# A 544-column pitch for the split activations, on a boundary of 256 bytes, in a hybrid decoder trunk

## The chip, the cores and the metric

The kernel runs on one core of one Trainium2 chip. The metric is the time of one execution on the device in microseconds. Of three runs of the kernel before, the median is 2366.6 us (2359.94, 2366.6 and 2373.5). No other core works beside it.

## The reference

A causal decoder trunk of two layers over 512 tokens with 16 learned tokens in front (528 positions, model width 1024, float32). Each layer is a SwiGLU feed-forward block, a token mixer, and a second SwiGLU block, each between two RMS norms:

```
h = concatenate([meta, x])
for layer in range(2):
    f = swiglu(rms_norm(h, nw[0]), w_gate, w_up, w_down)      # 1024 -> 2816 -> 1024
    h = h + 0.5 * rms_norm(f, nw[1])
    hn = rms_norm(h, nw[2])
    mix = even_mixer(hn) if layer == 0 else odd_mixer(hn)
    h = h + rms_norm(mix, nw[3])
    f = swiglu(rms_norm(h, nw[4]), w_gate, w_up, w_down)
    h = h + 0.5 * rms_norm(f, nw[5])
return h[:, 16:]
```

The even mixer is sliding-window attention beside a gated DeltaNet, with one input projection (1024 to 2824) and one output projection (1024 to 1024). The odd mixer is a gated linear attention in chunks (input 1024 to 3088, output 1024 to 1024). The four feed-forward blocks and the four projections hold most of the arithmetic.

## The kernel before, in words

**Layout.** The residual `h` lies transposed: 128 model columns on the partitions, eight such tiles (`DT` = 8), and the 528 tokens (`TOK`) along the row. All dense products are out = W^T h: a 128x128 block of weights is loaded into TensorE, and the tokens are streamed past it.

**Split operands.** TensorE reads both operands in the format fp32r. For precision each operand is kept as a high and a low part. The activations lie in `x_hl` (2 parts x 8 tiles x 528 columns), the hidden activations of a feed-forward block in `acts` (2 parts x 22 tiles x 528 columns), the weights in `w_hl` (a ring of four slots, 2 parts each). For each tile `kt` of the contraction `products` (L521) makes three products: high weights with high activations, high with low, low with high. Each is made once for every half of the tokens: columns 0 to 263 and 264 to 527. So one `kt` is six matmuls of 264 columns:

```
for part, moved in ((0, 0), (0, 1), (1, 0)):
    lhs = core.w_hl[:, slot.ring, part, w_tile * P:(w_tile + 1) * P]
    for b, (t0, n) in enumerate(halves(phase.cols)):
        op = pe.matmul(out, lhs, moving[:, moved, kt, t0:t0 + n], ...)
```

Where the first 16 tokens are no longer needed (layer 1 from the output projection on), a `kt` is three matmuls of 512 columns, from column 16 on.

**Slots.** A slot is one tile of 128 output columns (half of one in the down projection): 8 `kt` of `x_hl` in the gate, up, input and output projections, 11 `kt` of `acts` in each half of the down projection. SyncE loads its weights into `stage` (L510), ScalarE writes the high part (L446), VectorE the low part (L453), three slots ahead of TensorE. Semaphores count slots; each engine walks the same list of phases. ScalarE and VectorE also take each result out of PSUM: L970 to L989 and L793, L797 for the gate and up projection, which leave `acts`; L826, L829 for the down projection, which leave `f_down`; L968 for the input projections.

**Norms.** Between the phases `scalar_norm` and `vector_norm` work tile by tile: the scaled result of the phase before (`f_down` or `f_mix`) is added to `h` (L926), ScalarE writes the high part of `h` times the norm's weights into `x_hl` (L762), VectorE the low part (L917), and GpSimd adds squares (L1041).

**Places in SBUF.** The tiles are allocated one behind the other. `x_hl` starts at byte 100,000 of each partition (`x_at`), which is 160 beyond a multiple of 256, and its rows lie 528 x 4 = 2112 bytes apart, which is 64 beyond a multiple of 256. The low part starts 8 x 2112 = 16,896 bytes behind the high part, a multiple of 256. `f_down` lies over the high part of `x_hl` with the same pitch. The arena starts at byte 133,792, again 160 beyond a multiple of 256. It holds `acts`, and in other stages `f_mix`, the mixers' tiles, the constants' rows and `rows_x` and `rows_out`, the input and the output as they are in memory. The low part of `acts` starts 22 x 2112 bytes behind the high part, 128 beyond a multiple of 256. The weights in `w_hl` start at byte 33,408 and their blocks lie 512 bytes apart, so every block starts 128 beyond a multiple of 256.

Of the kernel before, what the change touches and what calls it, by code (L numbers as in the profile page):

```python
# [29 lines left out]
F32R = mybir.dt.float32r  # L30

P = 128
META = 16
SEQ = 512
TOK = META + SEQ
# [6 lines left out]
DT = D // P  # L42
# [23 lines left out]
SCALAR_LOADS = 6  # L66
VEC_ROWS = CONV * 3 * DH + 4 + 2 + 1
HALF = TOK // 2
FULL = "full"
TAIL = "tail"  # L70

# [57 lines left out]
class Phase:  # L129


    def __init__(self, kind, layer, slots, cols, before, ffn=None):
        self.kind, self.layer, self.slots, self.cols, self.ffn = kind, layer, slots, cols, ffn
        self.slot0 = before["slots"]

        self.partial = 0 if layer else slots - 1
        self.lead = 1 if kind == "in" and layer else 0
        self.evac0 = before["evac"]
        self.f0 = before["f"]
        self.x0 = before["x"]  # L140
        self.a0 = before["a"]
        before["slots"] += slots
        if kind in ("gu", "in"):
            before["evac"] += slots
        if kind == "gu":
            before["a"] += slots // 2
        if kind in ("down", "out"):
            before["f"] += DT
# [32 lines left out]
def plan(stop=None):  # L181
# [6 lines left out]
    def norm(layer, post, pre, half, cols, last=False):  # L188
        nonlocal norms, sums
        steps.append(("norm", Norm(layer, post, pre, half, cols, h0=norms * DT, x0=n["x"], sum0=sums,  # L190
                                   pair=(n["slots"] + RING - 1) % RING, last=last,
                                   sum_pair=(n["slots"] + (RING - 1 if half else RING - 2)) % RING)))
        norms += 1
        sums += (post is not None) + (pre is not None)
        if pre is not None:
            n["x"] += DT

    norm(0, None, 0, False, FULL)
    for layer in range(2):
        cols = FULL  # L200
        for ffn in range(2):
            if ffn:
                cols = TAIL if layer else FULL
            steps.append(("dense", Phase("gu", layer, 2 * FT, cols, n, ffn=ffn)))
# [7 lines left out]
            norm(layer, 1, 2, True, cols)  # L212
            steps.append(("dense", Phase("in", layer, (ODD_TILES if layer else EVEN_TILES) + 1, FULL, n)))
            steps.append(("mix", Mix(layer, n["x"], n["evac"], n["slots"])))
            n["x"] += DT
            steps.append(("dense", Phase("out", layer, DT, TAIL if layer else FULL, n)))
            if stop == (layer, "mix"):
                norm(layer, 3, None, False, TAIL if layer else FULL, last=True)
                return steps
# [4 lines left out]
def halves(cols):  # L224

    if cols == TAIL:
        return [(META, SEQ)]
    return [(0, HALF), (HALF, HALF)]


def token_cols(tile, cols):

    if cols == TAIL:
        return tile[:, META:TOK]
    return tile.rearrange("p (a b) -> p a b", a=2)
# [22 lines left out]
class Core:  # L258


    def __init__(self, nc, ctx, steps):
        self.nc, self.steps = nc, steps
        self.phases = [s for kind, s in steps if kind == "dense"]
        last = [s for kind, s in steps if kind == "norm"][-1]
        self.h_total = last.h0 + DT

        def sb(name, shape, dt=F32):
            return ctx.enter_context(nc.sbuf_tensor(name, shape, dt))

        def sem(name):  # L270
            return ctx.enter_context(nc.semaphore(name))

        self.h = sb("h", [P, DT, TOK])
        self.w_hl = sb("w_hl", [P, RING, 2, FH * P], F32R)
        self.stage = sb("stage", [P, 2, FH * P])
        self.rinv = sb("rinv", [P, TOK])
        self.sq_sum = sb("sq_sum", [P, TOK])
        self.t_gate = sb("t_gate", [P, TOK])
        self.t_up = sb("t_up", [P, TOK])
        self.ident = sb("ident", [P, P])  # L280
        self.ones = sb("ones", [P, P])
        self.norm_cols = sb("norm_cols", [P, 12 * DT])
        self.vec_cols = sb("vec_cols", [P, 64])
        self.heads = sb("heads", [P, QH + 2 * DH])
        self.eps = sb("eps", [P, 4])
        self.by_token = sb("by_token", [P, 2, 6])
        self.x_at = (nc.sbuf_base + 31) // 32 * 32
        self.x_hl = sb("x_hl", [P, 2, DT, TOK], F32R)
        self.arena = (nc.sbuf_base + 31) // 32 * 32
        self.acts = sb("acts", [P, 2, FT, TOK], F32R)  # L290
        self.psum = ctx.enter_context(nc.psum_tensor("psum", [P, 8, 512], F32))


        self.f_down = self.at("f_down", [P, DT, TOK], self.x_at)
        self.f_mix = self.at("f_mix", [P, DT, TOK], self.arena)

        at = self.arena
        def rows_at(name, rows, width):
            nonlocal at
            buf = self.at(name, [rows, width], at)  # L300
            at += (4 * width + 31) // 32 * 32
            return buf

        self.rows_x = rows_at("rows_x", P, NBLK * D)
        self.rows_meta = rows_at("rows_meta", META, D)
        self.rows_norm = rows_at("rows_norm", 12 * DT, P)
        self.rows_vec = rows_at("rows_vec", VEC_ROWS, P)
        self.table = rows_at("table", BUCKETS + 1, QH)
        self.bucket_hot = rows_at("bucket_hot", BUCKETS + 1, V_ALL)
        self.bias_row = rows_at("bias_row", QH, V_ALL)  # L310
        self.rows_x = self.rows_x[:].rearrange("p (b d) -> p b d", b=NBLK)
        self.rows_out = self.at("rows_out", [P, NBLK, D], self.arena)

        self.w_hi = sem("w_hi")
        self.w_lo = sem("w_lo")
        self.slot_used = sem("slot_used")
        self.scaled = sem("scaled")
        self.gate_silu = sem("gate_silu")
        self.act_full = sem("act_full")
        self.act_hi = sem("act_hi")  # L320
        self.act_lo = sem("act_lo")
        self.f_out = sem("f_out")
        self.sq_made = sem("sq_made")
        self.sq_added = sem("sq_added")
        self.sum_ready = sem("sum_ready")
        self.root_ready = sem("root_ready")
        self.rinv_ready = sem("rinv_ready")
        self.f_scaled = sem("f_scaled")
        self.f_scaled_pool = sem("f_scaled_pool")
        self.inverse_ready = sem("inverse_ready")  # L330
        self.spread_set = sem("spread_set")
        self.spread_ready = sem("spread_ready")
        self.spread_copied = sem("spread_copied")
        self.table_set = sem("table_set")
        self.h_new = sem("h_new")
        self.x_hi = sem("x_hi")
        self.x_lo = sem("x_lo")
        self.consts_in = sem("consts_in")
        self.vectors_in = sem("vectors_in")
        self.consts_set = sem("consts_set")  # L340
        self.cols_ready = sem("cols_ready")
        self.cols_flip = sem("cols_flip")
        self.tok_in = sem("tok_in")
        self.tok_flip = sem("tok_flip")
        self.bias_stored = sem("bias_stored")
        self.out_flip = sem("out_flip")
        self.out_left = sem("out_left")
        self.out_right = sem("out_right")
        self.out_stored = sem("out_stored")
        self.w_landed = [sem("w_landed_0"), sem("w_landed_1")]  # L350
        self.sem = sem
        self.tables = 0
        self.even = Even(self)
        self.odd = Odd(self)
        self.proj = [self.even.proj, self.odd.proj]
# [366 lines left out]
def bank_cols(core, pair, cols):  # L722
    if cols == TAIL:
        return core.psum[:, 2 * pair, 0:SEQ]
    return core.psum[:, 2 * pair:2 * pair + 2, 0:HALF]

# [218 lines left out]
def vector_dense(core, dve, phase):  # L945
    k = core

    def step(i, u):
# [9 lines left out]
        if phase.kind == "in":  # L958
# [5 lines left out]
            if slot.peeled:  # L964
                tile = k.proj[phase.layer][0:rows, at, :]
                src = k.psum[0:rows, 2 * slot.pair:2 * slot.pair + 2, 0:HALF]
                rinv = token_cols(k.rinv[0:rows, :], phase.cols)
# [1504 lines left out]
```

## Time and profile before

| | |
|---|---|
| median of three runs | 2366.6 us |
| profiled execution, its own time | 2361.65 us |
| its span, first to last instruction | 2359.9 us |
| TensorE busy with matmuls | 2250.8 us, 95% |
| VectorE, ScalarE, GpSimd busy | 1037.5, 749.6, 213.7 us |
| read from HBM | 175.64 MB, 75 GB/s |
| mean granted clock of TensorE | 0.976 of full |

Matmuls overlap in the records: one of 264 columns lasts some 284 ns from its start to its end, but the next one starts some 120 ns after it. So the rate is read from starts and counts, and not from the mean duration. A start is given to 0.01 us. A window on the time axis shows each instruction that is under way in it, with its true start.

### The profile page before, as it was taken

The page shows a single profiled execution, that of the slowest core. Times are in us where ns is not written, and L with a number is a line of the kernel's source. Part 1 is how long each engine was busy: PE and PEld are TensorE (multiplying, and loading weights), DVE is VectorE, ACT ScalarE, POOL GpSimd, SP SyncE. Part 2 cuts the span into 40 slices and gives each one's busy share as a digit, 9 for nine tenths or more (in the row PEclk, how much of TensorE's full clock was granted, in tenths as well). Part 3 has the DMA queues.
Part 4 walks back from the last instruction along what each step waited for, and adds up shares of the span by engine and source line. Part 5 has one row for each costly group of instructions (what it writes and reads, how often), then busy time and mean ns, then how long its engine had stood idle before and what let it go on. Part 6 is the DMA issues. An engine that isn't in the chain of part 4 may idle for free.

```text
span 2359.9 us, 38299 instructions
## 1 busy us (share of the span) xinstructions
PE 2250.8 (95%) x16046; PEld 2080.9 (88%) x16046; DVE 1037.5 (44%) x1298; ACT 749.6 (32%) x1103; POOL 213.7 (9%) x185
## 2 busy tenths in 40 slices
PE   7999999899969999999998999999899998999997
PEld 6999999788839889999998999999899776888885
DVE  5444422665454546444314544431564337444322
ACT  3322322344422433222222322222352454222321
POOL 2000000300044030000002000000200012000001
PEclk9999999998989999999999999999999999999998
DMA  3333332321100022333431333332132122333420
GB/s 104 98 89 90 104 108 72 74 66 46 46 9 2 1 72 81 89 89 89 117 88 36 95 92 89 96 111 72 40 92 72 45 75 60 98 89 98 119 86 36
DMA packets 347333, 179.02 MB, mean 76 GB/s; under 512 B 15657, under 2 KB 345680, under 8 KB 347246
## 3 DMA queue, kind: packets, MB, share of 16 engines
q1 hardware_dynamic: 346032, 175.30, 25.8%
q0 software_dynamic: 880, 2.34, 0.5%
q8 instruction: 65, 1.06, 0.2%
q14 instruction: 22, 0.18, 0.0%
q10 hardware_dynamic: 334, 0.14, 0.0%
HBM read 175.64 MB, written 2.12 MB: 75 GB/s over the span
## 4 chain that ended last, share of the span: by engine, by line
PE 89%; DVE 7%; ACT 2%; DMA 1%; issue 1%; POOL 0%; DVEq 0%; SPq 0%; ACTq 0%; POOLq 0%
PE psum L521 77%; DVE h L926 3%; DVE x_hl L917 1%; PE psum L1318 1%; ACT x_hl L762 1%; PE psum L1665 1%; PE psum L1681 1%; PE psum L1679 1%; PE psum L1337 1%; PE psum L646 1%; DMA stage<-even_w_in 0%; PE psum L2192 0%; PE psum L637 0%; PE psum L1351 0%; PE psum L1303 0%
## 5 line engine op out<-in xcount | busy, mean ns | idle before, releaser
L521 PE MATMUL psum<-x_hl,w_hl 128*128 128x264 f32 (+1 forms) x10272 | 1428.8, 301 | 42.7 <-DVE x_hl L917 39.4
L521 PEld LDWEIGHTS psum<-x_hl,w_hl 128*128 128x128 f32 x10272 | 1354.6, 191 | 118.4 <-issue 31.7
L453 DVE TENSOR_TENSOR w_hl<-stage,w_hl 128x1024 fp32r<-128x1024 f32 (+1 forms) x304 | 400.3, 1317 | 440.7 <-ACT w_hl L446 440.4
L521 PE MATMUL psum<-acts,w_hl 128*128 128x264 f32 (+1 forms) x3696 | 508.7, 300 | 0.0
L521 PEld LDWEIGHTS psum<-acts,w_hl 128*128 128x128 f32 x3696 | 484.6, 188 | 23.7
L446 ACT ACTIVATE w_hl<-stage 128x1024 fp32r<-128x1024 f32 (+1 forms) x304 | 338.5, 1114 | 226.1 <-PE psum L521 158.5
L976 DVE TENSOR_TENSOR t_up<-psum,rinv 128x528 f32<-128x528 f32 (+1 forms) x88 | 61.9, 703 | 306.6 <-PE psum L521 306.5
L797 ACT ACTIVATE acts<-t_up 128x528 f32 (+3 forms) x88 | 56.7, 644 | 401.1 <-DVE t_up L979 401.1
L970 DVE TENSOR_TENSOR t_gate<-psum,rinv 128x528 f32<-128x528 f32 (+1 forms) x88 | 61.8, 703 | 184.5 <-PE psum L521 184.4
L793 ACT ACTIVATE t_gate<-t_gate 128x528 f32<-128x528 f32 (+1 forms) x88 | 56.6, 643 | 249.5 <-DVE t_gate L970 249.5
L1037 POOL COPY sq_sum<-t_gate 128x528 f32<-128x528 f32 (+1 forms) x12 | 9.8, 818 | 1268.9 <-ACT t_gate L826 1262.3
L1041 POOL TENSOR_TENSOR sq_sum<-sq_sum,t_up 128x528 f32<-128x528 f32 (+1 forms) x42 | 59.3, 1411 | 226.8 <-ACT t_up L826 192.2
L1041 POOL TENSOR_TENSOR sq_sum<-sq_sum,t_gate 128x528 f32<-128x528 f32 (+1 forms) x36 | 51.4, 1428 | 219.4 <-ACT t_gate L826 189.9
L979 DVE TENSOR_TENSOR t_up<-t_up,t_gate 128x528 f32<-128x528 f32 (+1 forms) x88 | 62.0, 704 | 9.5
L989 DVE TENSOR_TENSOR acts<-t_up,acts 128x528 f32 (+3 forms) x88 | 61.4, 698 | 2.8 <-ACT acts L797 2.8
L826 ACT ACTIVATE t_gate<-psum 128x528 f32<-128x528 f32 (+1 forms) x24 | 14.6, 609 | 140.0 <-PE psum L521 140.0
L762 ACT ACTIVATE x_hl<-h,norm_cols 128x528 fp32r<-128x528 f32 (+1 forms) x48 | 35.2, 732 | 69.2 <-DVE h L926 69.2
L826 ACT ACTIVATE t_up<-psum 128x528 f32<-128x528 f32 (+1 forms) x24 | 14.5, 606 | 128.1 <-PE psum L521 128.1
L917 DVE SCALAR_TENSOR_TENSOR x_hl<-h,norm_cols,x_hl 128x528 fp32r<-128x528 f32 (+1 forms) x48 | 45.0, 949 | 19.1 <-ACT x_hl L762 19.1
L968 DVE TENSOR_TENSOR odd_proj<-psum,rinv 128x528 f32<-128x528 f32 (+1 forms) x25 | 17.5, 704 | 72.7 <-PE psum L521 72.7
L968 DVE TENSOR_TENSOR even_proj<-psum,rinv 128x528 f32<-128x528 f32 (+1 forms) x23 | 16.1, 705 | 64.6 <-PE psum L521 64.5
L926 DVE TENSOR_TENSOR h<-h,f_down 128x528 f32<-128x528 f32 x24 | 40.5, 1689 | 0.1
(311 smaller groups left out, 1342.1 us busy)
## 6 DMA issues: line engine op xcount, KB each, us to landing
stage<-ffn_w_gate SPq DMA_DIRECT2D x88, 512.0 KB, 3.8
stage<-ffn_w_up SPq DMA_DIRECT2D x88, 512.0 KB, 3.8
stage<-ffn_w_down SPq DMA_DIRECT2D x64, 704.0 KB, 4.6
stage<-odd_w_in SPq DMA_DIRECT2D x24, 512.0 KB, 3.8
stage<-even_w_in SPq DMA_DIRECT2D x18, 512.0 KB, 3.8
stage<-even_w_out SPq DMA_DIRECT2D x8, 512.0 KB, 3.6
stage<-odd_w_out SPq DMA_DIRECT2D x8, 512.0 KB, 3.8
rows_x<-x SPq DMA_DIRECT2D x1, 2048.0 KB, 10.4
```

The costliest lines, as they stand in the source:

```text
L446: act.activation(weights(core.w_hl[:, slot.ring, 0, :], *kind), weights(core.stage[:, slot.stage, :], *kind), ACT.Copy).then_inc(core.w_hi, 1)
L453: dve.tensor_tensor(weights(core.w_hl[:, slot.ring, 1, :], *kind), weights(core.stage[:, slot.stage, :], *kind), weights(core.w_hl[:, slot ...
L521: op = pe.matmul(out, lhs, moving[:, moved, kt, t0:t0 + n], start=first and part + moved == 0, stop=last and part == 1)
L762: act.activation(k.x_hl[:, 0, kt, norm.t0:TOK], tile, ACT.Copy, scale=k.norm_cols[:, col:col + 1]).then_inc(k.x_hi, 1)
L797: act.activation(token_cols(tile_at(k.acts[:, 0], t), phase.cols), token_cols(k.t_up[:, :], phase.cols), ACT.Copy).then_inc(k.act_hi, 1)
L917: dve.scalar_tensor_tensor(k.x_hl[:, 1, kt, t0:TOK], k.h[:, kt, t0:TOK], k.norm_cols[:, col:col + 1], k.x_hl[:, 0, kt, t0:TOK].bitcast(F32 ...
L926: dve.tensor_tensor(k.h[:, kt, t0:TOK], k.h[:, kt, t0:TOK], f[:, kt, t0:TOK], ALU.add).then_inc(k.h_new, 1)
L970: dve.tensor_tensor(token_cols(k.t_gate[:, :], phase.cols), src, rinv, ALU.mult).then_inc(k.scaled, 1)
L976: dve.tensor_tensor(up, src, rinv, ALU.mult).then_inc(k.scaled, 1)
L979: dve.tensor_tensor(up, up, gate, ALU.mult).then_inc(k.act_full, 1)
L989: dve.tensor_tensor(token_cols(tile_at(k.acts[:, 1], t), phase.cols), up, hi, ALU.subtract)\
L1041: pool.tensor_tensor(k.sq_sum[:, t0:TOK], k.sq_sum[:, t0:TOK], buf, ALU.add).then_inc(k.sq_added, 1)
```

## The change

The rows of `x_hl` are allocated 544 columns long (`PITCH`), of which the first 528 are used. 544 x 4 = 2176 bytes is 128 beyond a multiple of 256. A tile `x_gap`, which nothing reads or writes, fills the partition up to the next multiple of 256 bytes (`LINE`), so `x_hl` starts at byte 100,096. It takes 2 x 8 x 2176 = 34,816 bytes, a multiple of 256, so the arena starts on one too, at byte 134,912. `f_down` gets the pitch of `x_hl`, over which it lies. `acts` keeps its pitch of 528 columns. The weights stay where they are.

```
+PITCH = 544
+LINE = 256
...
+        self.x_gap = sb("x_gap", [P, (-nc.sbuf_base) % LINE // 32 * 8])
         self.x_at = (nc.sbuf_base + 31) // 32 * 32
-        self.x_hl = sb("x_hl", [P, 2, DT, TOK], F32R)
+        self.x_hl = sb("x_hl", [P, 2, DT, PITCH], F32R)[:, :, :, 0:TOK]
         self.arena = (nc.sbuf_base + 31) // 32 * 32
         self.acts = sb("acts", [P, 2, FT, TOK], F32R)
         self.psum = ctx.enter_context(nc.psum_tensor("psum", [P, 8, 512], F32))
 
 
-        self.f_down = self.at("f_down", [P, DT, TOK], self.x_at)
+        self.f_down = self.at("f_down", [P, DT, PITCH], self.x_at)[:, :, 0:TOK]
         self.f_mix = self.at("f_mix", [P, DT, TOK], self.arena)
```

Where the operands of the dense matmuls start, in bytes beyond a multiple of 256 (`kt` counted from the first row):

| | before | after |
|---|---|---|
| `x_hl`, first half, kt = 0, 1, 2, 3 | 160, 224, 32, 96 | 0, 128, 0, 128 |
| `x_hl`, second half | 192, 0, 64, 128 | 32, 160, 32, 160 |
| `x_hl`, 512 columns from column 16 | 224, 32, 96, 160 | 64, 192, 64, 192 |
| `acts` high, first half, kt = 0, 1, 2, 3 | 160, 224, 32, 96 | 0, 64, 128, 192 |
| `acts` high, second half | 192, 0, 64, 128 | 32, 96, 160, 224 |
| `acts` high, 512 columns from column 16 | 224, 32, 96, 160 | 64, 128, 192, 0 |

The low part of `x_hl` starts at the same places as the high part, the low part of `acts` 128 bytes further.

## Rows read from the trace of the kernel before

**Rows 1.** The page: TensorE's line, then the chain that ended last, by engine and line

```profile
PE 2250.8 (95%) x16046; PEld 2080.9 (88%) x16046; DVE 1037.5 (44%) x1298; ACT 749.6 (32%) x1103; POOL 213.7 (9%) x185
PE 89%; DVE 7%; ACT 2%; DMA 1%; issue 1%; POOL 0%; DVEq 0%; SPq 0%; ACTq 0%; POOLq 0%
```

**Rows 2.** That chain in order of time, merged: start us, us, what, xcount

```profile
50.01 368.10 PE psum L521 x3024
...
1305.64 368.11 PE psum L521 x3024
...
1980.67 351.58 PE psum L521 x1512
```

**Rows 3.** Stretches: length, busy us of engines (count), granted clock, DMA share, GB/s

```profile
901.00:1269.10 368.10, 368.10 (x3027) 368.10 (x3028) 138.22 (x148) 102.20 (x121) 8.63 (x7) 1.00 0.32 94
1269.10:1305.64 36.54, 27.56 (x181) 24.57 (x179) 26.81 (x27) 13.94 (x23) 13.70 (x10) 0.86 0.00 1
```

**Rows 4.** Groups of instructions, shapes apart: L521, count, busy us, mean ns, idle before

```profile
L521 PE MATMUL psum<-x_hl,w_hl 128*128 128x264 f32 x9024 | 1134.1, 288 | 35.0 <-DVE x_hl L917 31.9 <-DVE w_hl L453 1.0 <-DVE odd_proj L968 0.9
L521 PE MATMUL psum<-acts,w_hl 128*128 128x264 f32 x3168 | 385.8, 284 | 0.0
L521 PE MATMUL psum<-x_hl,w_hl 128*128 128x512 f32 x1248 | 294.7, 397 | 7.6 <-DVE x_hl L917 7.5 <-ACT rinv L732 0.2
L521 PE MATMUL psum<-acts,w_hl 128*128 128x512 f32 x528 | 123.0, 394 | 0.0
```

**Rows 5.** Instructions by time, TensorE: first matmuls of kt 0 to 4, one slot of `x_hl`

```profile
1405.00 0.40 PE L521 MATMUL psum<-x_hl,w_hl 128*128 128x264 f32 x2
1405.72 0.40 PE L521 MATMUL psum<-x_hl,w_hl 128*128 128x264 f32 x2
1406.45 0.42 PE L521 MATMUL psum<-x_hl,w_hl 128*128 128x264 f32 x2
1407.19 0.41 PE L521 MATMUL psum<-x_hl,w_hl 128*128 128x264 f32 x2
1407.92 0.40 PE L521 MATMUL psum<-x_hl,w_hl 128*128 128x264 f32 x2
```

**Rows 6.** The same for `acts`: first matmuls of kt 4, 6 and 8

```profile
1175.53 0.41 PE L521 MATMUL psum<-acts,w_hl 128*128 128x264 f32 x2
...
1176.99 0.41 PE L521 MATMUL psum<-acts,w_hl 128*128 128x264 f32 x2
...
1178.45 0.41 PE L521 MATMUL psum<-acts,w_hl 128*128 128x264 f32 x2
```

**Rows 7.** The same, `x_hl` with 512 columns: kt 0, 4, 6, 7, 8

```profile
2075.51 0.63 PE L521 MATMUL psum<-x_hl,w_hl 128*128 128x512 f32 x2
...
2078.30 0.62 PE L521 MATMUL psum<-x_hl,w_hl 128*128 128x512 f32 x2
...
2079.68 0.64 PE L521 MATMUL psum<-x_hl,w_hl 128*128 128x512 f32 x2
2080.39 0.62 PE L521 MATMUL psum<-x_hl,w_hl 128*128 128x512 f32 x2
2081.08 0.63 PE L521 MATMUL psum<-x_hl,w_hl 128*128 128x512 f32 x2
```

**Rows 8.** One line of ScalarE: duration ns min/median/max, first and last start

```profile
L762 ACT ACTIVATE x_hl<-h,norm_cols x48: 719/737/742, 22.6 to 1975.7; 128x528 fp32r<-128x528 f32 x40, 128x512 fp32r<-128x512 f32 x8
```

**Rows 9.** By time, one tile of a norm: VectorE's writes and GpSimd's add

```profile
1281.37 0.77 DVE L917 SCALAR_TENSOR_TENSOR x_hl<-h,norm_cols,x_hl 128x528 fp32r<-128x528 f32 x1 [0.19 <-ACT x_hl L762]
...
1281.95 1.36 POOL L1041 TENSOR_TENSOR sq_sum<-sq_sum,t_up 128x528 f32<-128x528 f32 x1 [0.91 <-ACT t_up L767]
...
1282.05 1.82 DVE L926 TENSOR_TENSOR h<-h,f_down 128x528 f32<-128x528 f32 x1
```

**Rows 10.** The start: landing of `x` (issued at 0.75 us), TensorE's first instruction

```profile
rows_x<-x SPq DMA_DIRECT2D x1, 2048.0 KB, 10.4
12.35 0.40 PE L658 MATMUL psum<-ident,rows_norm 96*128 96x96 f32 x1 [12.35 <-DMA heads<-dn_dt_bias]
```

## The prediction

> **What bounds the kernel now.** I read the page first. TensorE is busy 95% of the span, VectorE 44% and ScalarE 32%, and 89% of the chain that ended last runs over TensorE [rows 1]. The chain in order of time shows where: in four stretches it does not leave the dense matmuls of L521 at all. Three of these stretches hold 3024 matmuls of 264 columns each in 368.1 us (the first and the last of the three are in [rows 2]). The fourth holds 1512 matmuls of 512 columns in 351.58 us. That is 3 x 368.1 + 351.6 = 1455.9 us, 62% of the span. In such a stretch the granted clock is 1.00, the higher of the two levels (2.4 GHz), TensorE is busy all the time, and DMA works a third of it [rows 3]. So nothing there is waited for: the time is the number of matmuls times the distance from one to the next. Any change in that distance passes straight into the span. Between the stretches VectorE sets the time (26.81 of 36.54 us in the norm of [rows 3], with TensorE waiting for its tiles).
>
> The shapes kept apart give the counts [rows 4]: from `x_hl` 9024 matmuls of 264 columns and 1248 of 512, from `acts` 3168 and 528. The mean durations there overlap and are no distance. The distances come from starts. One slot of `x_hl` starts its `kt` at 1405.00, 1405.72, 1406.45, 1407.19 and 1407.92 [rows 5]: 0.72, 0.73, 0.74 and 0.73 us for six matmuls each, 2.92 us for four `kt`, 121.7 ns for a matmul. Four `kt` of `acts` also take 2.92 us (1175.53 to 1178.45), 1.46 for each two [rows 6]. With 512 columns four `kt` take 2.79 us (2075.51 to 2078.30), 232.5 ns for a matmul; of the next four, two take 1.38 together, then one 0.71 and one 0.69 [rows 7]. So the `kt` are not equal, though the instructions of each have the same shapes. What differs from one `kt` to the next is where the rows start, and that repeats after four of them. The trace thus has a hint that the start of a row plays a part, of 0.02 us in 0.73.
>
> **The change, part by part.** No instruction is added or taken away, and no wait, semaphore or transfer changes. What changes is the addresses of `x_hl`, `f_down` and all of the arena. So the sum has one kind of term: the number of instructions with a moved operand, times what the move is worth.
>
> *`x_hl`, 264 columns.* 9024 matmuls are 9024 / 6 = 1504 `kt`. Before, a quarter of them start at each of (160, 192), (224, 0), (32, 64) and (96, 128), first and second half, and take 0.72, 0.73, 0.74 and 0.73 us, as `kt` 0 to 3 of [rows 5]. After, half start at (0, 32) and half at (128, 160). The trace has neither pair. It has the four single places, though: the pair (0, 32) lies between (224, 0) and (32, 64), so I give it (0.73 + 0.74) / 2 = 0.735. The pair (128, 160) lies between (96, 128) and (160, 192), so it gets (0.73 + 0.72) / 2 = 0.725. Their mean is 0.730, that of before, and the term is 0. The bounds, by the nearest rows: all at the cheapest, 1504 x (0.72 - 0.73) = -15 us; all at the dearest, 1504 x (0.74 - 0.73) = +15 us. I take 0, since one new pair stands beside the dearest place and the other beside the cheapest.
>
> *`x_hl`, 512 columns.* 1248 / 3 = 416 `kt`, mean 0.697, dearest 0.71 and cheapest 0.69 [rows 7]. All starts of before are 32 beyond a multiple of 64, all starts of after (64, 192) are multiples of 64. With no row at such a start I take 0, with bounds from -3 to +5 us.
>
> *`acts`.* The pitch stays, and after as before each of four starts serves a quarter of the `kt`; the places only move by 96 bytes. Here the pairing of high and low part differs from that in `x_hl` (the low part starts 128 further on), and still four `kt` cost the same 2.92 us [rows 5, 6]. The mean over a full round of starts thus looks indifferent to how they follow each other. I take 0. The bounds, with half a hundredth of a microsecond of reading error on 3168 / 6 + 528 / 3 = 704 `kt`: -3.5 to +3.5 us.
>
> *The writers of `x_hl` and `f_down`.* ScalarE's L762 writes rows at all four starts, and its 48 durations lie within 719 to 742 ns, with both shapes in them [rows 8]. A shift of 12 ns in all 48 would be 0.6 us. VectorE's writes have a larger spread, but its cause stands beside them: the addition L926 takes 1.82 us where GpSimd's L1041 has begun 0.10 us before it and lasts 1.36, while the write of `x_hl` (L917), which meets no such neighbour, takes 0.77 [rows 9]. Addresses have no part in that. I take 0, from -1 to +1.
>
> *DMA.* `rows_x` lies in the arena. Its transfer is issued at 0.75 us and lands 10.4 us later, at 11.2, while TensorE's first instruction waits for a constant until 12.35 [rows 10]. A faster landing is hidden. A slower one is hidden up to 1.2 us, and costs its excess beyond that. The weights' loads go to `stage`, which is not moved, and TensorE waits for none of them in the long stretches. Term 0.
>
> *The mixers' tiles* move by 96 bytes with the arena and keep their shapes and pitches. All matmuls outside L521 are 16046 - 13968 = 2078, with other shapes; 1 ns on each is 2 us. Term 0, from -2 to +2.
>
> **The sum.** 0 + 0 + 0 + 0 + 0 + 0. The profiled execution took 2361.65 us for its span of 2359.9, which is 4.95 us under the median of the runs, 2366.6. I forecast that median again, to the full microsecond: 2366 us. The bounds added up are -25 and +27 us.
>
> **The rivals.**
>
> *Blocks (faster).* A read could cost by the aligned blocks of 64 bytes that it touches. 264 columns (1056 bytes) touch 17 at any multiple of 32, before and after. 512 columns (2048 bytes) touch 33 from a start that is 32 beyond a multiple of 64, and 32 from a multiple of 64. The two distances would then give (232.5 - 121.7) / 16 = 6.9 ns for a block, and the change saves one on each of 1248 + 528 = 1776 matmuls: -12.3 us, 2354 us. For it: the distances fit such a law, and all 512-column matmuls get an aligned start. Against it: they fit a price by column as well, since there are only two widths. The SBUF page of the Trainium skill ("SBUF — State Buffer", "Specifications (TRN2)") gives lines of 16 bytes. By that rule 512 columns touch as many lines before as after, and nothing is gained. No row here shows a line's size.
>
> *Kind places (faster).* The pairs (0, 32) and (128, 160) could both cost as the cheapest `kt`, 0.72: -15 us, 2351 us. For it: the pair that is that cheap now, (160, 192), contains one of the new places. Against it: the places 32 and 64 make the dearest pair, and 32 now serves a quarter of all reads instead of an eighth.
>
> *All of it alignment (much faster).* At 2.4 GHz 264 columns are 110.0 ns and 512 are 213.3, and the rows show 121.7 and 232.5. Were the surplus due to starts off a multiple of 256 and gone after: 12192 x 11.7 + 1776 x 19.2 = 177 us less, 2190 us. Against it: the `kt` of `x_hl` whose second half starts exactly at 0 takes 0.73, as much as one with starts at 96 and 128 and more than the one at (160, 192). On its own the page of the Trainium skill "TensorE: Matmul & The Clock Gate" ("Back-to-back issue gap") gives N/2.4 + 2.5 ns for the distance of warm matmuls, 112.5 and 215.8 ns here. The rows are 9.2 and 16.7 ns above it. By that rule the most that aligned starts could bring is 12192 x 9.2 + 1776 x 16.7 = 142 us, an estimate.
>
> *A clash that stays (slower).* A read of the tokens runs while the next block of weights is read, and all weights start at 128. A pair of starts could stand badly to that, as (32, 64) does, the dearest of [rows 5]. Of the new starts, 32 is in every second `kt`, and 128, on which the weights start too, leads the others. If both new pairs are dear for such a reason, all `kt` of 264 columns take 0.74: +15 us. The same on 512 columns, all at the dearest 0.71: 416 x 0.013 = +5 us. Together +20 us, 2386 us. For it: a pitch of 128 beyond 256 uses two places where 64 used four, so a bad one is no longer averaged out. Against it: 64 may be the bad one in its pair, and it is used no more in the halves; and 128 in second place costs 0.73, no more than the mean. It passes the line of 0.5% when the mean `kt` of 264 columns goes beyond 0.738 us.
>
> **How the numbers follow.** Of a change in this kernel 0.5%, some 12 us, can be told from none. No change has 0.61. Blocks has 0.09, kind places 0.09, all alignment 0.02; together 0.20 for faster. The clash that stays has 0.19. The range from 2348 to 2384 holds the forecast, the runs' own spread of 7 us to each side, blocks, kind places, and of the clash what makes one of the two new pairs dear, and most of what makes both. It leaves out the much faster case and the full clash with the 512 columns in it. The bounds of the unknown costs reach further, but only if every row falls on the same side.
>
> **What the profile after would show.** Right: the three stretches of 3024 matmuls at 368 us and the one of 1512 at 352, each within 1.5 us, and four `kt` of `x_hl` at 2.92 us, now with a pattern that repeats after two. Norm stretches stay at 36.5 us. Blocks: `kt` of 512 columns at 0.677 us and unchanged ones of 264. Kind places: 2.88 us for four `kt` of `x_hl`, and 2.92 for `acts`. Clash: 2.95 us or more for four `kt` of `x_hl`. I am wrong if the distance in `x_hl` leaves 121 to 122.5 ns, or if that of `acts` moves although each of its starts still serves a quarter.

## The result and the profile after

The changed kernel is slower by 0.39%: 2373.27 us median against 2364.14 before, eleven runs each, ratio 1.0039 with a 95% interval from 1.0023 to 1.0054. I had forecast 2366 us and no change. The time lies in the stated range, but the change is clear of the noise and is none that I called likeliest.

The page of the kernel after, TensorE's line and the chain by engine, as [rows 1] of before:

```profile
PE 2258.9 (96%) x16046; PEld 2091.0 (88%) x16046; DVE 1037.9 (44%) x1298; ACT 749.3 (32%) x1103; POOL 214.0 (9%) x185
PE 89%; DVE 7%; ACT 2%; DMA 1%; issue 0%; POOL 0%; ACTq 0%; DVEq 0%; SPq 0%; POOLq 0%
```

The counts are the same and only TensorE is busy longer, by 8.1 us. The chain in order of time (start us, us, what), as [rows 2], says where:

```profile
49.51 371.07 PE psum L524 x3024
...
904.75 371.07 PE psum L524 x3024
1312.44 371.04 PE psum L524 x3024
...
1989.90 348.56 PE psum L524 x1512
```

The same 3024 matmuls take 371.07 us instead of 368.10, three times, while the 1512 of 512 columns take 348.56 instead of 351.58. In sum +5.9 us in the long stretches. The stretch between the first two and the norm behind the second, by length, busy time of the engines, granted clock, DMA share and GB/s, as [rows 3]:

```profile
904.75:1275.82 371.07, 371.07 (x3027) 371.07 (x3028) 138.36 (x148) 102.00 (x121) 8.65 (x7) 1.00 0.32 93
1275.82:1312.44 36.62, 28.41 (x180) 25.61 (x179) 26.80 (x27) 13.94 (x23) 13.69 (x10) 0.81 0.01 1
```

The granted clock is 1.00 in both kernels and the other engines do what they did, so no wait and no lower clock lengthens the stretch. The norm is as long as before (36.62 and 36.54 us). What has changed is the distance from one matmul to the next. Here are the first matmuls of `kt` 0 to 4 of a slot of `x_hl`, as [rows 5]:

```profile
1413.11 0.41 PE L524 MATMUL psum<-x_hl,w_hl 128*128 128x264 f32 x2
1413.85 0.40 PE L524 MATMUL psum<-x_hl,w_hl 128*128 128x264 f32 x2
1414.59 0.41 PE L524 MATMUL psum<-x_hl,w_hl 128*128 128x264 f32 x2
1415.33 0.40 PE L524 MATMUL psum<-x_hl,w_hl 128*128 128x264 f32 x2
1416.07 0.41 PE L524 MATMUL psum<-x_hl,w_hl 128*128 128x264 f32 x2
```

Four `kt` take 2.96 us, each 0.74; before they took 2.92 (0.72, 0.73, 0.74, 0.73). With 512 columns, as [rows 7] but `kt` 0 to 4:

```profile
2083.82 0.62 PE L524 MATMUL psum<-x_hl,w_hl 128*128 128x512 f32 x2
2084.51 0.62 PE L524 MATMUL psum<-x_hl,w_hl 128*128 128x512 f32 x2
2085.20 0.62 PE L524 MATMUL psum<-x_hl,w_hl 128*128 128x512 f32 x2
2085.89 0.62 PE L524 MATMUL psum<-x_hl,w_hl 128*128 128x512 f32 x2
2086.58 0.62 PE L524 MATMUL psum<-x_hl,w_hl 128*128 128x512 f32 x2
```

Four take 2.76 us, before 2.79. The starts repeat so exactly that a slot is known to some nanoseconds. This is what a slot takes where TensorE waits for nothing (133 slots of `x_hl` with 264 columns and 45 with 512 in each trace), from its start to that of the next; `count` is the number of all such slots in the kernel:

```
slot                                before      after     count   difference
x_hl, 264 columns (48 matmuls)     5.840 us   5.920 us     188     +15.0 us
x_hl, 512 columns (24)             5.573      5.520         52      -2.8
acts, 264, halves of a tile (66)   8.026, 8.028   8.029, 7.991   24 each   -0.8
acts, 512, halves of a tile (33)   7.675, 7.678   7.626, 7.624    8 each   -0.8
sum                                                                  +10.6
```

Not every slot is the common one: in the kernel after 124 of the 133 take 5.920 us, and five in a row, in the input projection of layer 1, take 5.867. With the mean of the 133 the first term is +14.5 us. The medians of the two kernels differ by 9.1 us. The two profiled executions differ by only 4.7 us in their spans: 188 counts also the slots of the input projections, where TensorE waits for others in between and part of a longer slot is hidden, and the stretches with waits vary by a few microseconds from run to run.

### The profile page after: what moved, and what is told of

Its sections match the earlier page's. It is cut to its first block, busy times and chain, and to the rows that moved or that the text cites. A ratio compares the mean times of both kernels' runs of the same rounds, so it can differ in the third digit from the quotient of the medians.

```text
span 2364.6 us, 38299 instructions
## 1 busy us (share of the span) xinstructions
PE 2258.9 (96%) x16046; PEld 2091.0 (88%) x16046; DVE 1037.9 (44%) x1298; ACT 749.3 (32%) x1103; POOL 214.0 (9%) x185
## 4 chain that ended last, share of the span: by engine, by line
PE 89%; DVE 7%; ACT 2%; DMA 1%; issue 0%; POOL 0%; ACTq 0%; DVEq 0%; SPq 0%; POOLq 0%
PE psum L524 77%; DVE h L929 3%; DVE x_hl L920 1%; PE psum L1321 1%; ACT x_hl L765 1%; PE psum L1668 1%; PE psum L1684 1%; PE psum L649 1%; PE psum L1682 1%; PE psum L1340 1%; DMA stage<-even_w_in 1%; PE psum L1306 0%; PE psum L2195 0%; PE psum L640 0%; PE psum L1354 0%
## 5 line engine op out<-in xcount | busy, mean ns | idle before, releaser
L829 ACT ACTIVATE t_up<-psum 128x528 f32<-128x528 f32 (+1 forms) x24 | 14.5, 605 | 127.4 <-PE psum L524 127.4
## 6 DMA issues: line engine op xcount, KB each, us to landing
rows_x<-x SPq DMA_DIRECT2D x1, 2048.0 KB, 10.6
```

## The experiments

My theory after this result, "places": the distance between two matmuls depends on where in 256 bytes the reads of the tokens start. Two rivals: the neighbours at work in SBUF stretch it, or it is the pitch as such, two places in place of four.

**The matmuls by themselves.** A kernel that only streams matmuls, in the order of `products`, from tiles at chosen bytes (`s` is the start of the first read beyond a multiple of 256, the second read follows 1056 bytes on):

```
+for part, moved in ((0, 0), (0, 1), (1, 0)):
+    for b, (s, n) in enumerate(kt):
+        pe.matmul(psum[:, b, 0:n], wt[w][:, part, (i % 8) * P:(i % 8 + 1) * P], tile[:, at:at + n], ...)
```

> Leaves the whole trunk out: it only streams matmuls of the changed kernel's kind (three products for each of 8 kt, two halves of 264 columns, every weight block 128 bytes beyond a multiple of 256) from tiles that start at chosen bytes. Its output is not the trunk's. Theory 'places': the distance between matmuls is a function of where the reads of the tokens start, modulo 256 bytes, and of nothing else in the kernel. Then the case with the starts of the kernel before takes 5.84 us for 48 matmuls and the case with those of the kernel after 5.92, as in the two traces, with no other engine at work. Rival 'neighbours': the distance is stretched by what VectorE, ScalarE and DMA do in SBUF at the same time; then both cases come out alike here, and under 5.84. Of the cases with one pair of starts throughout I expect by 'places' (0, 32) and (128, 160) at 5.90 to 5.95 and some pair at or below 5.80. The cases with the weights at 0 instead of 128 tell whether the place counts by itself or against the weights' place: if against it, the row of eight pairs is the same but turned by 128 bytes (0 and 128 change places); if by itself, it is the same row unturned. 256 and 272 columns in place of 264 and 264: by 'places' the second read then starts where the first does, modulo 256.

The trace of that kernel by time: start, us, and what TensorE does. `before_x` and `after_x` have the starts of the two kernels, with the weights at 128:

```profile
50.17 6.00 PE L100 MATMUL psum<-before_x,w_mid 128*128 128x264 f32 x48
56.01 6.04 PE L100 MATMUL psum<-after_x,w_mid 128*128 128x264 f32 x48
61.89 46.68 PE L100 MATMUL psum<-pair_x,w_mid 128*128 128x264 f32 x384
```

From start to start 5.84 us for the layout of before, exactly as in the kernel, and 5.88 for that of after: in its second half the `kt` take 0.74 us each as in the kernel, in the first half they are still finding that pace. VectorE and GpSimd do nothing here, and ScalarE next to nothing, so the neighbours are out. Then eight starts, each for 48 matmuls, first with the weights at 128 (`w_mid`) and then at 0 (`w_zero`); each row is the first of a start:

```profile
61.89 0.41 PE L100 MATMUL psum<-pair_x,w_mid 128*128 128x264 f32 x2
67.81 0.40 PE L100 MATMUL psum<-pair_x,w_mid 128*128 128x264 f32 x2
...
79.35 0.40 PE L100 MATMUL psum<-pair_x,w_mid 128*128 128x264 f32 x2
85.12 0.40 PE L100 MATMUL psum<-pair_x,w_mid 128*128 128x264 f32 x2
90.88 0.40 PE L100 MATMUL psum<-pair_x,w_mid 128*128 128x264 f32 x2
...
102.53 0.41 PE L100 MATMUL psum<-pair_x,w_mid 128*128 128x264 f32 x2
108.41 0.41 PE L100 MATMUL psum<-pair_x,w_zero 128*128 128x264 f32 x2
114.17 0.40 PE L100 MATMUL psum<-pair_x,w_zero 128*128 128x264 f32 x2
...
125.83 0.41 PE L100 MATMUL psum<-pair_x,w_zero 128*128 128x264 f32 x2
131.71 0.41 PE L100 MATMUL psum<-pair_x,w_zero 128*128 128x264 f32 x2
137.63 0.41 PE L100 MATMUL psum<-pair_x,w_zero 128*128 128x264 f32 x2
...
149.18 0.40 PE L100 MATMUL psum<-pair_x,w_zero 128*128 128x264 f32 x2
154.95 0.41 PE L100 MATMUL psum<-same_x,w_mid 128*128 128x264 f32 x2
```

The differences of the starts, the rows left out included, in microseconds for 48 matmuls:

```
start of the first read      0     32    64    96    128   160   192   224
weights at 128             5.92  5.76  5.77  5.77  5.76  5.80  5.86  5.88
weights at 0               5.76  5.80  5.86  5.88  5.92  5.78  5.77  5.77
```

The second line is the first turned by 128, to 0.02 us. So a start is neither good nor bad by itself: what counts is how far beyond the weights' start it lies, modulo 256. Best are the same place and the 96 bytes below it: the starts 32, 64, 96 and 128 all settle at 120 ns for a matmul, which is 288 cycles at 2.4 GHz. On the weights' place itself every single matmul of the settled half follows after 120 ns. Worst is 128 beyond (5.92 us). The changed kernel has every second `kt` of `x_hl` exactly there, its first reads at 0 against weights at 128. One half of my expectation failed: I had (128, 160) at 5.90 or more, and by itself it is among the best, 0.720 us for a `kt`. In the changed kernel, between two `kt` at (0, 32), it takes 0.738. So a `kt` beside the bad start is dear too; why it is, no run isolates.

The same trace has three more sets. In eight streams both reads of a product start at the same byte: 5.92, 5.84, 5.79, 5.77, 5.83, 5.86, 5.81 and 5.84 us for the starts 0 to 224. So the second read counts as well: with both exactly on the weights' place a slot takes 5.83 us, with the second 32 bytes beyond it 5.76. With 512 columns, 24 matmuls take 5.46 us on the weights' place, 5.51 from a start 64 beyond it, and 5.60 to 5.62 from the other six. With 256 and 272 columns the five starts gave 5.77 to 5.87, no better.

**The pitch alone.** As the change, without the gap ahead of `x_hl`:

```
-        self.x_gap = sb("x_gap", [P, (-nc.sbuf_base) % LINE // 32 * 8])
```

> Pitch 544 without the gap: x_hl starts at byte 100,000 (160 beyond 256) and its kt start in turn at (160, 192) and (32, 64). Theory 'places' takes these from the kernel before, 0.722 and 0.744 us for a kt: 5.87 us for a slot of 48 matmuls, so 188 slots x 0.03 = +5 us against before, about half of what the full change costs. Rival 'pitch' (two places instead of four are what costs, whichever they are): 5.92 us for a slot as after the full change, +15 us from these matmuls and the same +9 us in the median.

Its chain in order of time:

```profile
50.59 367.01 PE psum L524 x3024
...
1981.05 352.65 PE psum L524 x1512
```

A slot of `x_hl` takes 5.813 us, less than before the change, 5.600 with 512 columns. Both theories missed. It is not the pitch, and it is not the mean of single places: the `kt` from (32, 64) takes 0.744 us in the kernel before, where others follow it, and 0.725 here. The time is 2363.25 us, ratio 0.9983 to before (0.9971 to 0.9995), some 4 us less, and the slots say 3.6.

**The aligned start alone.** `PITCH = 528`, the gap stays:

```
-PITCH = 544
+PITCH = 528
```

> x_hl and the arena begin on a multiple of 256, but the pitch stays 528 columns: kt in turn at (0, 32), (64, 96), (128, 160) and (192, 224). Theory 'places': (0, 32) and (128, 160) keep the 0.742 and 0.738 us that they have after, the others are not known in x_hl; with these near the mean of before (0.73) a slot takes 5.88 us, +7 us. Rival 'pitch': four places are used again, so a slot is back at 5.84 and the time at that of before. By both, acts stay as they are after the full change (8.03 and 7.99 us for a half slot of 66, before 8.03 both).

```profile
50.59 367.85 PE psum L524 x3024
...
899.05 369.19 PE psum L524 x3024
1303.09 369.19 PE psum L524 x3024
...
1980.42 350.22 PE psum L524 x1512
```

Time 2364.69 us, ratio 1.0000 (0.9985 to 1.0015). The three first stretches run the same instructions on the same rows of `x_hl`, against weights that all start at 128, and still the first is 1.3 us shorter: its slots take 5.840 us, those of the other two 5.873. So one layout can run in two rhythms, as in the kernel after (5.920 and 5.867 us). The slots of `acts` are those of after (8.029 and 7.991 us), which puts the small gain of `acts` on the arena's start alone. The two parts of the change do not add up, either: -3.6 us for the pitch and +1.9 for the start in the slots' sums, +10.6 for both. It is where all the reads start together that counts.

**The weights moved.** The full change, with only the weights shifted:

```
+        self.w_gap = sb("w_gap", [P, 56])
         self.w_hl = sb("w_hl", [P, RING, 2, FH * P], F32R)
```

The small tiles between `w_hl` and `x_hl`, which no dense matmul reads, move by 224 bytes with the weights; `x_gap` then puts `x_hl` and the arena 256 bytes on, so their starts modulo 256 stay.

> The changed kernel with a gap of 224 bytes ahead of w_hl, and nothing else: the activations keep their starts of after (0 and 128, second halves 32 and 160), the weights' blocks now start 96 beyond a multiple of 256 instead of 128. Theory 'against the weights': only the distance between the two starts counts, modulo 256. It is then 160 and 32 for x_hl, as in the kernel with the pitch alone, and for acts as in the kernel before: a slot of x_hl takes 5.81 us instead of 5.92, a half slot of acts 8.03, and the time falls by 188 x 0.107 - 48 x 0.017 - 52 x 0.080 (512 columns back at 5.60) - 0.8 = 14 us, to some 4 us under the kernel before. Rival 'own place': what counts is the activations' start by itself: then all stays as after, 5.92 us for a slot and +9 us on the kernel before.

```profile
51.49 367.11 PE psum L525 x3024
...
1974.92 352.72 PE psum L525 x1512
```

A slot of `x_hl` takes 5.813 us (after 5.920), with 512 columns 5.600, a half slot of `acts` 8.027 and 8.033: in the four kinds the figures of the kernel with the pitch alone, to 6 ns, though no activation lies where it lay there. The time is 2360.07 us, ratio 0.9971 (0.9958 to 0.9984). That decides against the activations' own place, in the kernel itself: 224 bytes ahead of the weights turn the slower kernel into one faster than before.

**Layouts in streams.** 58 layouts (the expectation miscounts them as 51) of 96 matmuls of 264 columns, of 256 and 272 in turn, or 48 of 512:

```
+    hi = (s + pitch * kt) % 256
+    low = (s + lo + pitch * kt) % 256
```

> Leaves the trunk out, as the streams before: 96 matmuls of 264 columns (or 48 of 512) for each of 51 layouts, weights at 128, with the starts stepping by 64, 128 or 0 bytes from one kt to the next, from several first places and with the low part 0, 64, 128 or 192 beyond the high. By 'against the weights' the best layout is the one with every start on the weights' place (step 0, from 128): 288 of TensorE's 2.4 GHz cycles for a matmul, 11.52 us for 96, and 546 cycles for 512 columns, against 11.68 us for the steps of before. Steps of 64 from 0 with the low part 0 should give 11.72 us (the kernel with the aligned start alone has 5.862 for 48), steps of 128 from 0 11.84, from 32 11.63. What is open is whether the cost is the mean of single places (then every first place of a step of 64 gives within 0.3% of the same) or depends on the order in which they follow (then they differ by more).

Each row is the first of a layout: steps of 128 from 0, 16, 32 and 48, then no step from 128 and what follows it, then 512 columns with no step from 128 and what follows it:

```profile
250.27 0.41 PE L117 MATMUL psum<-p128from_x,w_mid 128*128 128x264 f32 x2
262.01 0.41 PE L117 MATMUL psum<-p128from_x,w_mid 128*128 128x264 f32 x2
273.68 0.40 PE L117 MATMUL psum<-p128from_x,w_mid 128*128 128x264 f32 x2
285.30 0.41 PE L117 MATMUL psum<-p128from_x,w_mid 128*128 128x264 f32 x2
...
402.29 0.40 PE L117 MATMUL psum<-p256from_x,w_mid 128*128 128x264 f32 x2
413.82 0.41 PE L117 MATMUL psum<-p256from_x,w_mid 128*128 128x264 f32 x2
...
483.38 0.63 PE L117 MATMUL psum<-full256from_x,w_mid 128*128 128x512 f32 x2
494.29 0.62 PE L117 MATMUL psum<-full256from_x,w_mid 128*128 128x512 f32 x2
```

Steps of 128 from 0 take 11.74 us, from 16 11.67, from 32 11.62. No step, on the weights' place, takes 11.53 (120 ns each). No step from 112 and from 160 is as good (11.52 and 11.54), from 144 it takes 11.73; so with 264 columns the weights' place is one of the best, and not the only one. With 512 columns no step on the weights' place takes 10.91 us for 48, 544 cycles each once settled against 557 in the kernel before. Sixteen layouts with steps of 64 take 290.7 to 293.7 cycles for a matmul in their second half, a spread of 1%. The four that start from 0 read the same places and differ by as much (290.7 to 293.7), so it is not only the set of places that counts. How they are paired and ordered may be the reason, or what ran just before: each layout was run once, one behind the other. One figure missed: steps of 128 from 0, the layout of after, should have had 11.84 us (296 cycles) and had 293.3.

**The same layout, entered in different ways.**

> Leaves the trunk out. Streams of 96 matmuls in four layouts (starts of the kernel after, of before, of the pitch alone, of the aligned start alone), each entered from a standstill, from the even stream with every start on the weights' place, from that with 512 columns, and from another uneven stream; then with the true steps over 1024 bytes in place of 256. The streams before had 296 cycles for the layout of after in one run (as in the kernel, 5.92 us for 48) and 293.3 in the next (5.87). Theory 'history': the same layout settles in one of several rhythms, depending on how it is entered; then the four entries differ. Rival 'address above 256': a step or a place beyond 256 bytes counts; then the four entries agree and the 1024 version differs from them.

By time, start and length of each stream (the length holds the last one's end, so the next start less this one's is the better measure):

```profile
49.28 11.69 PE L113 MATMUL psum<-one_place_x,w_mid 128*128 128x264 f32 x96
60.81 12.00 PE L113 MATMUL psum<-after_from_one_x,w_mid 128*128 128x264 f32 x96
72.65 11.07 PE L113 MATMUL psum<-one_wide_x,w_mid 128*128 128x512 f32 x48
83.56 11.98 PE L113 MATMUL psum<-after_from_wide_x,w_mid 128*128 128x264 f32 x96
95.38 11.87 PE L113 MATMUL psum<-other_x,w_mid 128*128 128x264 f32 x96
107.08 11.90 PE L113 MATMUL psum<-after_from_other_x,w_mid 128*128 128x264 f32 x96
```

The layout of after takes 11.84 us (60.81 to 72.65) when entered from the even stream, and its settled half has 296 cycles for a matmul. Entered from another uneven stream it has 293.35, `kt` of 0.736 and 0.731 us instead of 0.742 and 0.738. So it has two rhythms. They are those of the kernel after: 124 of its 133 slots without a wait run in the slower one, and five at 5.867 us, which is 293.35 cycles, in the faster. The layouts of before and of the pitch alone gave one rhythm from all four entries (292.0, 290.7); that of the aligned start alone again two (292.0, 293.7). The version with the true steps over 1024 bytes took 293.35 for the layout of after from a standstill, where the one over 256 took 296. This run does not decide between the two theories. Each entry reads a tile of its own, so the addresses above 256 were not held fixed: by the kernel's allocations the first three tiles (296 cycles) lie 4608 bytes apart, which is 9 x 512, and the fourth (293.35) a further 4864, which is 9.5 x 512. The stream of the same layout in the run before, with 293.35 cycles, lies like the fourth. An address modulo 512 would sort these streams as well as their history does, though it does not sort those of the aligned start alone. That one set of addresses can have both rhythms is shown by the trunk: `x_hl` lies still, and its slots take 5.840 or 5.873 us with the aligned start alone, 5.867 or 5.920 in the kernel after. What chooses between them stays open.

**A layout on the weights' place.** Rows 2304 bytes apart, starting at 128 as the weights do:

```
+PITCH = 576
+        self.x_gap = sb("x_gap", [P, (128 - nc.sbuf_base) % LINE // 32 * 8])
...
+        self.norm_second = self.at("norm_second", [P, 6 * DT], gap + 13 * ROW)
+        self.heads = self.at("heads", [P, QH + 2 * DH], gap + 14 * ROW)
...
-        self.wide3 = at("dn_wide3", [P, DH * P], x + 3 * big)
+        self.wide3 = at("dn_wide3", [P, DH * P], free + 27840 + 4608 + 960)
```

> The layout that the streams point to: rows of x_hl 576 columns apart (2304 bytes, a multiple of 256) and starting 128 beyond a multiple of 256, exactly where the weights' blocks start, so every first half reads from the weights' place and every second half 32 bytes beyond it. To make room the small tiles heads, eps, by_token and the norm columns of layer 1 lie in the unused ends of two rows, and one mixer tile moves into the arena's free end. The arena starts at 192, so acts step through the places 0, 64, 128, 192 as in the changed kernel. By 'against the weights': a slot of x_hl 5.76 us (before 5.84, after 5.92), that is -15.0 us over 188 slots; with 512 columns, which start 64 beyond the weights' place, 5.51 (before 5.57), -3.5 us over 52; acts -1.6 us as after. Sum -20 us: 2345 us, 0.85% under the kernel before. Rival 'the rest gives it back' (the waits outside the long stretches, some 464 us of the span, take up what TensorE gains, since its consumers and loads set them): then the long stretches shorten as said and the time falls by less than 10 us.

```profile
50.84 364.25 PE psum L528 x3024
...
1968.28 351.98 PE psum L528 x1512
```

2345.73 us, ratio 0.9916 to before (0.9896 to 0.9936). The slot of `x_hl` takes 5.760 us as said, the slots of `acts` gave 2.4 us in place of 1.6. With 512 columns, where the reads start 64 beyond the weights' place, my 5.51 us held for five slots of the output projection only (5.493). The 40 of the last feed-forward block take 5.600, 0.03 more than before; the mean is 5.59. So this layout too has two rhythms, and the streams had shown only the faster (549.4 cycles, 5.49 us for 24). The slots sum to -16.7 us and the medians differ by 18.4, so nothing is given back elsewhere.

**The wide reads too.** Where 512 tokens are left they lie from column 0 on, and so start on the weights' place (the instructions that write `x_hl` there follow; they are not shown):

```
+    skip = META if phase.cols == TAIL and moving is core.x_hl else 0
...
-            op = pe.matmul(out, lhs, moving[:, moved, kt, t0:t0 + n], start=first and part + moved == 0,
+            op = pe.matmul(out, lhs, moving[:, moved, kt, t0 - skip:t0 - skip + n], start=first and part + moved == 0,
```

> The last layout again, and where only 512 tokens are left, x_hl holds them from column 0 instead of 16, so that these reads too start on the weights' place and not 64 beyond it. In the last run they took 5.59 us for a slot of 24 matmuls, where I had expected 5.51; so the even streams are not a safe guide for a start beside the weights' place. On the place itself all streams so far had a single rhythm, 544 cycles. By 'against the weights' a slot with 512 columns takes 5.44 us: 52 x 0.15 = -8 us on the last kernel, 2338 us, 1.15% under the kernel before. Rival 'streams mislead': in the kernel a stream on the weights' place has a second, slower rhythm as well; then these slots stay at 5.55 us or more and the time near 2345 us.

```profile
49.65 364.25 PE psum L529 x3024
...
1963.34 345.46 PE psum L529 x1512
```

2339.27 us, ratio 0.9896 (0.9879 to 0.9912): 24 us under the kernel before it in the same comparison, and the slots sum to -24.4. The slot with 512 columns takes 5.440 us, all 45 of them. The rival, a second and slower rhythm on the place itself, did not show. This is the best version that I ran.

## Why the prediction was wrong

- *What bounds the kernel.* Right. The long stretches are the number of matmuls times their distance, and every change of the distance went into the span.
- *`x_hl`, 264 columns: the step that failed.* I gave each new pair the mean of its two neighbours in the trace, 0.735 and 0.725 us, and so the term 0. The trace after has 0.742 and 0.738, and the term is +15.0 us, the upper bound that I had named. The distance is 123.3 ns, outside the 121 to 122.5 that I had set as a sign of being wrong. Two assumptions in that term were false. One is that the cost belongs to a pair of places: the same (32, 64) took 0.744 us before and 0.725 with the pitch alone. The other is that it changes smoothly from place to place: against weights at 128 the start 0 takes 5.92 us for 48 and the start 32 takes 5.76, side by side. The third fact I had on the page and did not use in the sum: all weights start at 128. The change put the first reads of every second `kt` just half of 256 bytes from them. The `kt` between, which I had at 0.725 and which takes 0.720 by itself, became dear beside them (0.738).
- *`x_hl`, 512 columns.* Forecast 0 within -3 and +5 us, measured -2.8.
- *`acts`.* Forecast 0 within 3.5 us, measured -1.6. That the mean over four starts is indifferent to how they follow each other was too strong: moved by 96 bytes, the same steps gain 0.2% at 264 columns and 0.7% at 512.
- *Writers, norms, DMA, mixers.* Held at 0, as far as the runs tell: the norm takes 36.5 and 36.6 us and ScalarE's and VectorE's busy sums agree within 0.4 us.
- *The rivals.* "A clash that stays" was right where it counts: it priced all `kt` at 0.74 us, +15 us, and the trace has that. Its mechanism, the reads against the weights, was also the one that the experiments bore out, though I had suspected 32 and 128 and it was 0. Its second part, 512 columns dearer by 5 us, was wrong. "Blocks" asked for 0.677 us for a `kt` of 512 columns and unchanged ones of 264; they were 0.690 and dearer. By the lines of 16 bytes of the Trainium skill ("SBUF — State Buffer", "Specifications (TRN2)"), of which both widths touch as many before as after, neither would have moved. The slots of 512 columns got 1% shorter and those of 264 got 1.4% longer, so a count of lines gives neither. "Kind places" and "all of it alignment" fell with the first row of the trace after. Aligned starts as such bring nothing: the changed kernel had them and was slower. From the formula of the Trainium skill for an isolated gap ("TensorE: Matmul & The Clock Gate", "Back-to-back issue gap") 112.5 and 215.8 ns follow as an estimate for the two widths. The best layout here still has 120.0 and 226.7, and the measurement decides. Of the 11.7 ns that a matmul of 264 columns has above its columns' 110.0, 1.7 went away on the weights' place, and of the 18.9 with 512 columns 5.5.
- *The chance.* I gave a slower time by more than 0.5% 0.19 and a change within it 0.61. The measured 0.39% lies within, but the centre of my forecast was a sum of zeros over unknown terms of up to 15 us, and the only row that varied showed that the term was alive.

## What to carry to other kernels

Where TensorE is never waited for and its matmuls are short, look at starts and not at durations: a pattern that repeats with the addresses means that the placement in SBUF is a term of the time. Place the moving operand by the stationary one, its first read on the same byte modulo 256 and with rows a multiple of 256 apart, rather than on a round address. Here, with the second read 32 bytes further on, that was worth 1.0%. A round start alone brought nothing, and together with rows of 544 columns it cost 0.4%. Where rows can't have such a pitch, try places against the trace, since neither a mean over places nor a stream of its own forecast them all.

## What the runs showed of the hardware that I had not expected

- In fp32r streams with a weight load for every matmul, the distance between matmuls of 264 columns is 288 to 296 cycles at the granted 2.4 GHz (starts on multiples of 16 bytes), by the moving starts less the weights' start modulo 256. Of 512 columns it is 544 to 563 with steps of 0, 64 or 128 bytes, and 568 with no step from 112. The figures are 288.0 and 544.0, with no variation from one `kt` to the next, where the first read is on the weights' place and the second, with 264 columns, 32 beyond. With both reads of 264 columns on the place it is 291.7.
- Small shifts count, and not smoothly. With both reads on one start and the weights at 128, 264 columns took 296.1 cycles on a multiple of 256, 303.5 from 4 bytes beyond it, 296.3 from 8 and 288.1 from 16. Each is one stream. The start 4 beyond is dearer than all others, the one 8 beyond, also no multiple of 16, is not.
- The same reads of `x_hl` can settle in two rhythms. In the kernel after they are 293.35 and 296.0 cycles. With the aligned start alone one stretch takes 367.85 us and two equal ones 369.19. What chooses the rhythm, and which unit of SBUF makes 256 bytes the period, no run here shows.
